# Gate rows spread by DMA, queries computed feature-major, adaLN sums on VectorE, and token lists built on the chip, in a hybrid mLSTM and attention layer with routed experts

## The reference, cut to what matters

```python
h = rmsnorm(x, norm_mix) * (1 + sc1) + sh1         # sh, sc, g: silu(c) @ w_ada + b_ada, six parts
p = h @ w_in                                       # 3600 columns: q,k,v,o of 4 mLSTM heads, 16 gates, q,k,v of 4 attention heads
# mLSTM, both directions, chunks of 128 tokens; b = cumsum(log_sigmoid(f)), ig = input gate
dmat = where(causal, b[:, None] - b[None, :] + ig[None, :], -inf)
m_t = maximum(b + m, max(dmat)); w_intra = exp(dmat - m_t)
s = (q @ k.T) * w_intra
num = s @ v + exp(b + m - m_t) * (C @ q);  h = num / maximum(abs(den), exp(-m_t))
# differential attention, then
x = x + g1 * (concat(head norms) @ w_out)
h = rmsnorm(x, norm_ffn) * (1 + sc2) + sh2
lg = h @ w_rg + b_rg ; grp = argmax(lg)            # 4 groups
le = (h @ w_re + b_re)[grp] ; top 2 of 4 experts   # softmax weights
y = sum over chosen experts of weight * ((silu(a) * u) @ w_dn[e]),  a, u = split(h @ w_gu[e])
x = x + g2 * y ; out = rmsnorm(x) * final_norm
```

## Time and profile before

| what | value |
|---|---|
| median of 3 runs | 817.06 us (814.7 to 818.93) |
| profiled execution | 812.73 us, span 811.0 us |
| PE busy | 696.1 us (86%), 2640 matmul records |
| DVE, ACT, POOL busy | 320.5, 172.6, 108.3 us |
| chain that ended last, by engine | PE 76%, DVE 10%, DMA 5%, issue 4% |
| mean granted clock of PE | 0.944 |

### The profile page before, as it was taken

How to read it: one execution, slowest core, us unless ns; L and a number is a source line. 1 busy time by engine, 2 the same in 40 slices (tenths; PEclk the granted TensorE clock), 3 DMA queues, 4 the chain that set the end, 5 groups by cost and what they waited for, 6 DMA issues and landing times.

```text
span 811.0 us, 7471 instructions
## 1 busy us (share of the span) xinstructions
PE 696.1 (86%) x2640; PEld 354.5 (44%) x2640; DVE 320.5 (40%) x680; ACT 172.6 (21%) x407; POOL 108.3 (13%) x146
## 2 busy tenths in 40 slices
PE   3799999899999999997788989972499999999900
PEld 1443453335555555543566644541244444444400
DVE  2332262121443532456898254566120211112038
ACT  5000200001111111111567411211021111212133
POOL 1321000011010100002162200102200111110040
PEclk9999999999999999999899999995699999999955
DMA  8997413803030030303100377000289999999373
GB/s 293 386 355 234 144 64 115 301 1 117 18 113 0 2 116 0 104 0 108 49 1 1 131 256 288 27 26 27 77 286 347 360 369 349 366 340 348 133 269 145
DMA packets 58057, 135.18 MB, mean 167 GB/s; under 512 B 4962, under 2 KB 6202, under 8 KB 58028
## 3 DMA queue, kind: packets, MB, share of 16 engines
q1 hardware_dynamic: 46992, 107.08, 37.1%
q0 software_dynamic: 5632, 15.65, 5.4%
q10 hardware_dynamic: 5404, 12.06, 3.8%
HBM read 119.98 MB, written 14.76 MB: 166 GB/s over the span
## 4 chain that ended last, share of the span: by engine, by line
PE 76%; DVE 10%; DMA 5%; issue 4%; SPq 3%; ACT 2%; DVEq 0%; POOLq 0%; POOL 0%; ACTq 0%
PE PS L1326 29%; PE PS L1614 14%; PE PS L1527 8%; PE PS L1629 7%; DMA PR<-in_w_ada 3%; PE PS L1358 2%; PE PS L1581 1%; PE PS L1420 1%; PE PS L1414 1%; PE PS L1516 1%; DVE stat L1064 1%; DVE PR L936 1%; PE PS L1446 1%; PE PS L1607 1%; PE PS L1348 1%
## 5 line engine op out<-in xcount | busy, mean ns | idle before, releaser
L1326 PE MATMUL PS<-RING,hT 128*128 128x512 f32 x560 | 253.0, 599 | 1.3 <-DVE hT L895 1.3
L1326 PEld LDWEIGHTS PS<-RING,hT 128*128 128x128 f32 x560 | 102.6, 191 | 122.7 <-issue 121.8
L1614 PE MATMUL PS<-PR,RING 128*128 128x512 f32 x256 | 113.2, 595 | 0.1
L1527 PE MATMUL PS<-RING,hT 128*128 128x512 f32 x160 | 72.4, 608 | 0.0
L1614 PEld LDWEIGHTS PS<-PR,RING 128*128 128x128 f32 x256 | 47.4, 190 | 55.3 <-issue 53.6
L1629 PE MATMUL PS<-PR,RING 128*128 128x512 f32 x128 | 57.6, 592 | 0.0
L1527 PEld LDWEIGHTS PS<-RING,hT 128*128 128x128 f32 x160 | 30.3, 194 | 35.4 <-issue 35.3
L1206 DVE COPY RING<-PS 128x512 f32<-128x512 f32 x32 | 20.6, 687 | 55.5 <-PE PS L1607 54.9
L1211 DVE TENSOR_TENSOR RING<-RING,PS 128x256 f32<-128x256 f32 x16 | 6.8, 422 | 77.3 <-ACT RING L808 77.3
L1629 PEld LDWEIGHTS PS<-PR,RING 128*128 128x128 f32 x128 | 23.7, 190 | 26.8 <-issue 26.8
L1607 PE MATMUL PS<-ident,RING 128*128 128x128 f32 x128 | 18.6, 293 | 18.4 <-DMA RING<-scratch_h,idp 15.6
(11 more groups left out here) (289 smaller groups left out, 881.3 us busy)
## 6 DMA issues: line engine op xcount, KB each, us to landing
PR<-in_w_gate_up SPq DMA_DIRECT2D x16, 2048.0 KB, 10.1
PR<-in_w_ada SPq DMA_DIRECT2D x20, 1024.0 KB, 13.2
PR<-in_w_down SPq DMA_DIRECT2D x16, 1024.0 KB, 12.3
RING<-in_w_in SPq DMA_DIRECT2D x14, 1024.0 KB, 7.3
scratch_y<-RING ACTq DMA_DIRECT2D x16, 512.0 KB, 8.1
RING<-in_w_ada SPq DMA_DIRECT2D x4, 1024.0 KB, 13.1
RING<-in_w_out SPq DMA_DIRECT2D x4, 1024.0 KB, 6.8
scratch_h<-HM ACTq DMA_DIRECT2D x5, 512.0 KB, 2.6
```

The costliest lines, as they stand in the source:

```text
L1326: last = mm(PS[:, m % 2, :], hTv[:, k, t * P:(t + 1) * P], ring[:, ci % 2, k, :], start=(k == 0), stop=(k == KD - 1))
L1527: last = mm(PS[:, i % 4, :], hTv[:, k, t * P:(t + 1) * P], ring[:, (WOUT + q) % 2, k, :], start=(k == 0), stop=(k == KD - 1))
L1614: last = mm(PS[:, 4 + b, :], xgT[:, b, k, :], gub[b][:, k, :], start=(k == 0), stop=(k == KD - 1))
```

## The change

1. **Gates** in four column groups; DVE adds four partial sums.
2. **Queries of the mLSTM feature-major.** For the chunk mq the weights are the stationary operand and `hT` the moving one; the result goes straight into `mqT`, cut in five units of 512 columns of the flattened [head, token] axis. The transposes and DVE copies of mq go.
3. **adaLN sum.** `ada2_sum` and DVE's two copies go; DVE adds the four row groups of PSUM onto the bias row. Bias rows are loaded after the store of the row before in that buffer; the next adaLN job waits for the sum.
4. **Gate broadcast.** SP stores `gf` to HBM and loads for each pass a [4 heads, 128 tokens] piece onto all partitions (`mbuf`, two buffers), in line with its weight chunks. POOL adds the mask there, ACT reads it. Both matmuls into bank 5 and `mdiag` go.
5. **Routing.** Logits with the tokens as stationary operand, so that they come out token-major; bias by DVE. `route` takes the best two experts of all groups at once. Residual, square, modulation, transposes and copies in halves; `place` is cut in three; the order on DVE and PE is new. h2's stores move from ACT's queue to SP's.
6. **Token lists.** DVE compares each token's rank with 0..127 (`rmat`), PE multiplies that with token numbers (`pid`) and DVE sums over the tiles into `idall`. The scatter, the zeroing and the load of `scratch_ids` go. For further rounds the list is built again at the end of each, in PE's loop, now nested.

```diff
@@ SP
+        def load_mb(g):
+            d, t = MG[g]
+            if g == 0:
+                sp.wait_ge(gf_stored, 16)
+                sp.wait_ge(gate_step, 3)
+            if g >= 2:
+                sp.wait_ge(w_ready, g - 1)
+            src = scratch["gfr"][:, d * T + t * P:d * T + (t + 1) * P]
+            sp.dma_start(mbuf[:, g % 2], src.partition_broadcast(P)).then_inc(mb_in[g % 2], 16)
...
             if ci == 4:
                 load_ada2(8)
+                sp.wait_ge(gate_step, 2)
+                sp.dma_start(scratch["gfr"], gf.rearrange("p d t -> p (d t)")).then_inc(gf_stored, 16)
...
+            for g in MB_AFTER.get(ci, ()):      # {5: (0, 1), 6: (2, 3), 7: (4, 5, 6), 8: (7, 8, 9)}
+                load_mb(g)
...
+        for t in range(NT):
+            sp.wait_ge(h2_ready, 2 * (t + 1))
+            sp.dma_start(scratch["h2"][t * P:(t + 1) * P, :], h2[:, t % 2, :]).then_inc(h2_stored[t % 2], 16)
@@ POOL
-            nc.gpsimd.tensor_tensor(mdiag, gf[:, d, t * P:(t + 1) * P].unsqueeze(1).broadcast_to([H, H, P]),
-                                    eye4[:, 0, :].unsqueeze(2).broadcast_to([H, H, P]), ALU.mult).then_inc(mdiag_ready, 1)
+            pool.wait_ge(mb_in[g % 2], 16 * (g // 2 + 1))
+            nc.gpsimd.tensor_tensor(mbuf[:, g % 2], mbuf[:, g % 2], masks[:, d, :].unsqueeze(1).broadcast_to([P, H, P]),
+                                    ALU.add).then_inc(mb_ready, 1)
@@ DVE, adaLN
-            V.tensor_copy(adp2[0:ROWS4 - 1, n_ % 2, :], PS[0:ROWS4 - 1, 4, :]).then_inc(ada_part, 1)
+            for g in range(3):
+                step(V.tensor_tensor(row, PS[32 * g:32 * g + 2, 4, :], row, ALU.add))
+            last = V.tensor_tensor(row, PS[96:98, 4, :], row, ALU.add)
@@ DVE, output projection
+        for t in range(NT):
+            if t >= 2:
+                place_rank(t - 2)
+            residual(t, 0)
+            if t >= 2:
+                place_id(t - 2)
+                place_slot(t - 2)
+            if t >= 1:
+                route(t - 1)
+            residual(t, 1)
+            if t == NT - 1:
+                place_rank(t - 1)
+            modulate(t)
+        place_id(NT - 2)
+        place_slot(NT - 2)
+        route(NT - 1)
+        place_rank(NT - 1)
@@ PE, mq
+                for k in ks:
+                    h, lo, hi, o = spans[hf % len(spans)]
+                    last = mm(PS[:, m % 2, o:o + hi - lo], ring[:, ci % 2, k, h * P:(h + 1) * P], hTv[:, k, lo:hi],
+                              start=(k == 0), stop=(k == KD - 1))
@@ PE, mLSTM loop
-            mm(PS[:, 5, :], identb[:], masksb[:, d, :].unsqueeze(1).broadcast_to([P, H, P]), start=True, stop=False)
-            mm(PS[:, 5, :], ones4[:], mdiag.rearrange("p h t -> p (h t)"), start=False, stop=True).then_inc(mb_done, 1)
@@ PE, output projection
+        for t in range(NT):
+            lo = 4 if t < 2 else 0
+            mid = (lo + KD) // 2
+            for q in range(2):
...
+                oproj(t, q, lo, mid)
+                if q == 0 and t >= 2:
+                    ranks(t - 2)
+                if q == 1 and t >= 1:
+                    logits(t - 1)
+                oproj(t, q, mid, KD)
+                if q == 0 and t >= 2:
+                    pe.wait_ge(rm_ready, t - 1)
+                    slot_ids(t - 2)          # 2 matmuls: PS[:, 6, 32:48] <- rmat, pid
+                if q == 0 and t >= 1:
+                    h2_transpose(t - 1)
+        ranks(NT - 2)
+        pe.wait_ge(rm_ready, NT - 1)
+        slot_ids(NT - 2)
+        h2_transpose(NT - 1)
+        logits(NT - 1)
+        ranks(NT - 1)
+        pe.wait_ge(rm_ready, NT)
+        slot_ids(NT - 1)
```

More of the change, by code:

```diff
@@ L250, in build_body @@
     kw_ready = sem("kw_ready")
-    mdiag_ready = sem("mdiag_ready")
-    mb_done = sem("mb_done")
+    mb_in = [sem(f"mb_in{b}") for b in range(2)]
+    mb_ready = sem("mb_ready")
     int_done = sem("int_done")
@@ L687, in _ @@
             for h in range(H):
-                ins = nc.scalar.activation(wexp[:, g % 2, h, :], PS[:, 5, h * P:(h + 1) * P], ACT.Exp,
+                ins = nc.scalar.activation(wexp[:, g % 2, h, :], mbuf[:, g % 2, h, :], ACT.Exp,
                                            bias=gcol[:, 0, d, t, h:h + 1], scale=-1.0)
@@ L1186, in _ @@
-        for k in range(2, ROUNDS):
-            step(V.scalar_tensor_tensor(cnt[:, 1:2], cnt[:, 0:1], float(k * P), cnt[:, 1:2], ALU.is_gt, ALU.add))
-        step(V.tensor_copy(rnd[:], cnt[:, 1:2]))
+        place_id(NT - 1)
+        step(V.tensor_scalar(rt[:, 9, 0, :], misc[:, 42:46], cnt[:, 0:1], None, ALU.is_lt))
+        step(V.tensor_reduce(cnt[:, 1:2], rt[:, 9, 0, :], AX.X, ALU.add))
+        step(V.tensor_scalar(rnd[:], cnt[:, 1:2], 1.0, None, ALU.add))
         dve.sem_inc(rounds_ready, 1)
+        place_slot(NT - 1)
@@ new lines, in h2_transpose, with logits @@
+        def h2_transpose(t):
+            if t == 0:
+                pe.wait_ge(omix, NT)
+            for k2 in range(2):
+                pe.wait_ge(h2_ready, 2 * t + k2 + 1)
+                if t >= 1:
+                    pe.wait_ge(h2T_ready, 2 * (t - 1) + k2 + 1)
+                for k in range(4 * k2, 4 * k2 + 4):
+                    last = tr(PS[:, 4 + k2, (k % 4) * P:(k % 4 + 1) * P], h2[:, t % 2, k * P:(k + 1) * P], ident[:])
+                last.then_inc(h2_T, 1)
+        def logits(t):
+            if t >= 1:
+                pe.wait_ge(lg_ready, t)
+                pe.wait_ge(id_read, t)
+            for k in range(KD):
+                if k % 4 == 0:
+                    pe.wait_ge(h2T_ready, 2 * t + k // 4 + 1)
+                last = mm(PS[:, 6, 0:20], hTv[:, k, t * P:(t + 1) * P], wroute[:, k, :], start=(k == 0), stop=(k == KD - 1))
+            last.then_inc(logit_done, 1)
@@ new lines, in ranks, with slot_ids @@
+        def ranks(t):
+            pe.wait_ge(oh_ready, t + 1)
+            for j in range(t + 1):
+                last = mm(PS[:, 7, NE * t:NE * t + NE], masksb[:, 2 if j == t else 3, :], ohb[:, j, :],
+                          start=(j == 0), stop=(j == t))
+            if t == NT - 1:
+                for j in range(NT):
+                    last = mm(PS[:, 7, 80:96], masksb[:, 3, :], ohb[:, j, :], start=(j == 0), stop=(j == NT - 1))
+            last.then_inc(rank_done, 1)
+        def slot_ids(t):
+            for j in range(2):
+                last = mm(PS[:, 6, 32:48], rmat[:, t % 2, j, :], pid[:, t, j, :], start=(j == 0), stop=(j == 1))
+            last.then_inc(ids_done, 1)
@@ L1601, in _ @@
             pe.sem_inc(dn_done[b], 1)
[L1602 removed]
+        with pe.Fori(0, n_rounds) as r:
+          with pe.Fori(0, PAIRS) as q8:
+            it = r * PAIRS + q8
             for b in range(2):
@@ L1637, in _ @@
                 last.then_inc(dn_done[b], 1)
+          for t in range(NT):
+            pe.wait_ge(rm_ready, r * NT + (NT + t + 1))
+            slot_ids(t)
 _INS = ["x_prompt", "x_sample", "cache_k", "cache_v", "state_C", "state_n", "state_m", "c", "c_ctx", "w_ada", "b_ada",
```

356 lines of the change are left out of this document (173 added, 183 removed).

## The result

| | before | changed kernel |
|---|---|---|
| median, device us | 816.25 (814.7 to 818.93, 4 runs) | 781.1 (778.9 to 782.72, 4 runs) |
| profiled execution, span | 812.73, 811.0 | 778.9, 777.1 |
| mean granted clock of PE | 0.944 | 0.946 |

The ratio is 0.956, with an interval of 0.953 to 0.960: 35 us faster. A second set of six runs on another chip gave 782.14 against 816.07, ratio 0.960 (0.956 to 0.964). The forecast was a median of 786 and a profiled execution of 781.4.

What follows compares the result with a forecast made beforehand. It took PE to bind the projection stage, mLSTM loop and output projection, and one serial lane the routing tail. Terms -10.9 - 13.6 + 4.5 - 11.3 = -31.3 us gave about 781.4 profiled, median 786, own range 780 to 792.

Steps and rivals of the forecast that it cites:

- the 12.5 of the sum: Projection stage: gates 2.1, adaLN sums 8.8 and q transposes 2.3, less 0.7 for feature-major q, in us saved.
- The longer wait: Projection stage: PE's wait for adaLN weights grows from 2.5 to 4.1 us, leaving a gain of 10.9.
- the fourth tile's logits: Output projection: these logits move ahead of the last projection, plus 1.9 us.
- the compare's wait in the third tile: Output projection: DVE's rank compare ends at 8.75 where PE asks at 7.05, plus 1.7 us.
- the first tile's halves: Output projection: the first tile's h2 comes in halves, so PE's wait of 2.41 shrinks by about 1.2 us.
- +0.7 for each of three tiles: Output projection: token placing 0.5 us, and logits at 2.1 instead of 1.9, 2.1 in all.
- The rival of the exposed loads: Output projection logits: 128-column weight loads not covered by 20-column matmuls, 7 us in all, total 793; chance 0.02.
- the 28.0: Routing tail: us from the end of the last projection to the first expert transposes, instead of 39.3.
- the store can't overtake: Output projection: h2's stores on SP's queue land behind the expert weights, near 504 and 506, costing nothing.
- Routing as the bound: Rival: routing lane has 0.15 us room per tile; 2.5 longer costs 9.5 in all, total 795.5; chance 0.12.
- The broadcast: Rival, mLSTM loop: PE waits for weights via SP, DMA, POOL and ACT; none of 13.6 us kept, 799.5; chance 0.09.
- that nothing changes: Rival, whole kernel: gate groups run serially, DVE's sums and lists hold PE as long as its matmuls did; 816, chance 0.02.

Runs made afterwards that it cites:

- E10: The changed kernel, unedited, timed again on another chip as base for further runs; median 782.14 us, ratio 0.960 to the kernel before.
- E3: The changed kernel with SP issuing the weights of adaLN job 9 one chunk earlier; median 775.61 us, ratio 0.954 to the kernel before.
- E4: The changed kernel with four unused f32 matmuls on PE ahead of adaLN job 9, where PE waits for weights; median 783.06 us.
- E1: The kernel before with items 1 to 4 of the change alone, routing as before; median 790.46 us against 815.05, ratio 0.973.
- E8: The changed kernel with POOL's wait for the slots moved from before the first gather to before the final picks; median 782.12 us.
- E5: The changed kernel with twelve unused dependent one-element copies added to each route on DVE; median 794.21 us, ratio 0.973 to the kernel before.
- E6: The changed kernel with one gate broadcast buffer instead of two, each load waiting for the previous pass's exponential; median 781.16 us, ratio 0.959.
- E7: The changed kernel with PE's token placing put behind the transposes of the next h2 instead of ahead; median 780.87 us.

## Why the prediction was right

The mechanism and the sum held: -31.3 forecast, -33.9 in the span. The sum is closer than its terms, which is luck: the projection fell short by 1.2, while the loop, the output projection and the tail were each 0.8 to 1.5 better than forecast. Of the 4.9 us between 786 and 781.1, 2.5 are terms, and 2.4 are the step from the profiled execution to the median: 4.3 was added as for the kernel before, and this time the median lay only 2.2 above it. That step depends on which execution was profiled; in E10 the profiled one took 782.64, 0.5 more than the median.

**Projection, -10.9; measured -9.7.** Gates: -2.1 as worked out. The removed work is more than the 12.5 of the sum: with the wait gone (E3) the stage is 15.8 shorter than before without its first mask block; 2.5 of that is the old wait, 13.3 the work. One part is the adaLN sum: a projection unit with its job takes 9.33 (59.46 to the next job at 68.79) where it took 10.47, so 1.14 for each of eight in place of 1.1; the rest, 0.5, was not split. The longer wait was foreseen (4.1, measured 4.49). The step that was missing is the clock: PE stood still for 4.5 and the next job took 3.37 instead of 1.90, which E3 and E4 pin on the stop. The granted clock is 0.56 while it runs (140.3 to 143.7), which is mostly the lower of the two levels, and 1.00 again from 144 to 150. Behind the old wait of 2.50 the job had taken 1.90. The Trainium skill, "TensorE: Matmul & The Clock Gate", section "Part 1: The HAM clock gate", tells of a clock that drops to half when PE has idled; the trace agrees, with 1.47 lost behind this stop.

**mLSTM loop, -13.6; measured -14.7.** The size was off: each pass is 1.47 shorter, not 1.36. Before, the score matmuls of the first passes started 18.76 and 19.19 apart (the third at 228.62), after 17.29 and 17.72 (179.93, 197.22, 214.94). PE of the kernel before, first passes and, for the next part, output projection:
```profile
190.67 1.16 PE L1420 MATMUL PS<-PR 128*128 128x128 f32 x8
...
209.43 1.16 PE L1420 MATMUL PS<-PR 128*128 128x128 f32 x8
...
483.78 5.29 PE L1527 MATMUL PS<-RING,hT 128*128 128x512 f32 x8
489.00 1.92 PE L1581 MATMUL PS<-hT,wroute 128*20 128x128 f32 x16
490.86 7.13 PE L1527 MATMUL PS<-RING,hT 128*128 128x512 f32 x16
...
523.06 1.92 PE L1581 MATMUL PS<-hT,wroute 128*20 128x128 f32 x16
```
The block itself was 1.36; the other 0.11 is the score row, 1.05 after, 1.16 before. It now follows f32 records over 128 partitions and no longer the matmul over four; why that makes it shorter was not tried. The ninth pass keeps its wait, as said:
```profile
331.67 1.16 PE L1518 MATMUL PS<-PR,TMP 128*128 128x129 f32 x8 [0.99 <-DVEq L1052]
```
POOL's mask addition takes 1.27 in most passes, not 1.03, and costs nothing.

**Output projection, +4.5; measured +3.0.** By terms: the fourth tile's logits +1.9, measured 1.7; the compare's wait in the third tile +1.7, measured 1.60; the first tile's halves -1.2, measured -0.74 (2.41 against 1.00 + 0.67). The term that failed is +0.7 for each of three tiles: a steady tile costs nothing more (17.05 against 17.04). Placing token numbers does take 0.46 (473.28 to 473.74), but from the logits' start to the next row is 1.70 (479.78 to 481.48) where it was 1.86 (489.00 to 490.86), against the +0.2 that was priced, and the transposition of the logits (0.17 per tile), which the tail's sum counted out, was forgotten here. The rival of the exposed loads is refuted: with 128 weight columns and 20 moving ones the row is 0.16 shorter, not 1.4 longer. This is not because the loads are short. The weight loads of such a row, before and after:
```profile
506.02 1.65 PEld L1581 LDWEIGHTS PS<-hT,wroute 128*20 128x20 f32 x16 [0.76 <-issue]
```
```profile
479.78 1.75 PEld L1645 LDWEIGHTS PS<-wroute,hT 128*128 128x128 f32 x15 [0.24 <-issue]
```
A load took 100 ns on average before and 192 after (PEld rows from 500 to 530 and from 476 to 500). The Trainium skill, "TensorE: Matmul & The Clock Gate", section "LDWEIGHTS (loading the stationary operand)", which the prediction weighed, lets the time of a load grow with its weight columns, and the trace agrees. What fails is to add that growth to the matmuls: loads run beside them. They were busy for 1.52 of 1.80 us before (489.00 to 490.80) and for all of 1.64 after (479.81 to 481.45), while each matmul now streams 20 columns instead of 128. So the loads fill this row by now, and it is no longer than they are. The terms as measured give 2.6 of the 3.0. A low clock behind the wait costs another 1.47 in the third tile's projection (5.07 against 3.60), but before had such a stretch too (5.29 behind its 2.41), so it hardly shows in the difference: E1 and E3 have none, and differ by the same 3.0 (84.6 and 87.6).

**Routing tail, -11.3; measured -12.1 (28.0 against 27.0).** The lane reached the second transposes at 6.1 instead of 6.2, the logits took 3.44 at half clock instead of 4.0. Route took 3.82 from the start of L1138 to its end at 533.55, as forecast (3.8), and rank matmuls, compare and placing took 2.5 instead of 2.75. The clock stayed low, as assumed (0.56 from 519 to 547). Slots and gather followed as summed. The tail is 1.0 shorter than the 28.0 and yet only 0.8 better than the -11.3, because the table cuts before's last projection at 540.2 and the prediction at 540.0. What the sum did not ask is whether the gather must stand behind the slots at all: E8 says no, and the tail is 2.2 shorter.

**Expert loop and end, 0.** The loop kept its length and its seam waits of 0.4; the end's list was covered with 4.2 to spare, against 1 to 4. The stores of h2 landed in 12.9, then in 5.8, 2.9, 2.6 and 2.6, and nobody waited for them. The prediction's "the store can't overtake" says more than its source. The Trainium skill, "DMA: Bandwidth & Descriptors", section "Queues, rings and completion order", has the descriptors of a ring taken up in order, but a later one may finish its write before an earlier one. No run here tests which holds for such a store.

**Rivals.** Routing as the bound: the room of 0.15 was right, and E5 shows what its loss costs, more than the rival had priced: 2.35 per tile and 2.5 in the tail for a lane longer by 2.5, while E5's 2.2 cost 3.95 in each of the last two tiles and 4.4 in the tail. The broadcast (E6) and the exposed loads (the logits row) are refuted; that nothing changes is refuted by the three stages that fell.

## What to carry to other kernels

Where an engine is busy for 98% of a stage, count what leaves it by its pitch, from one start to the next, neighbours included; here 1.1 was counted for a measured 1.14, and 1.36 for a measured 1.47, where the difference sat in a neighbour's row. Then look for the loads and waits whose place in another engine's program was tuned to the old length: a wait for something that lands at a fixed time grows by what was saved ahead of it, and on PE it can also take clock from the work behind. An edit of 2 us that the median hides can still be judged by cutting both traces at the same events, and several such edits together show in the median.

## What was not expected of the hardware

What a stop of PE costs at a lower granted clock behind it does not follow from its length. A stop of 1.60 cost another 1.47 (5.07 for 3.60, granted clock 0.72 from 475 to 480), and so did one of 4.49 (3.37 for 1.90). Nor is it always due. In E3 the same stop as the first, 1.59, was followed by eight records in 3.60, and so it was in E8 (1.61), where four records behind the first tile's stops had taken 3.19 for 1.88 (granted clock 0.56) instead. E3's rows:
```profile
467.49 0.62 PE L1663 MATMUL PS<-TMP 128*128 128x16 f32 x4 [1.59 <-DVE TMP L1172]
...
468.86 3.60 PE L1600 MATMUL PS<-RING,hT 128*128 128x512 f32 x8
```
The kernel before took 5.29 behind its stop of 2.41, E1 with the same code 3.60 behind 2.40. So about half of E7's gain hangs on whether the clock falls there. After 0.38 in E7 and 1.00 in the ninth pass the rows kept their full-clock length. The clock can also fall where PE doesn't stop: in E7's profile it was granted at 0.81 from 113 to 122, behind the thin transposes of the chunk ends, while PE was busy for all of these 9.00 us, and from the job at 80.54 to the one at 122.07 that cost 1.7 against the changed kernel. What decides was not found.

Much of the spread between executions comes from stretches that no edit touched: ahead of the projection the profiled executions took 40.3 to 44.3 with the same instructions. Of the 3.7 between the changed kernel's two spans (777.1 and 780.8) 3.3 lie there. The table of stretches, from 32 to 40 us, shows these two, the shorter one first:
```profile
32.00:40.00 8.00, 6.77 (x52) 3.40 (x44) 1.65 (x5) 0.00 (x0) 5.79 (x9) 0.87 1.06 388
```
```profile
32.00:40.00 8.00, 6.53 (x31) 2.83 (x28) 1.16 (x2) 0.00 (x0) 7.09 (x11) 0.50 1.08 372
```
The weights arrive at 388 and 372 GB/s, and the clock is at its lower level in one (0.50) and mostly at the upper in the other (0.87). Why it differs was not tried.
